# Two norms of a chained FFN and attention block: scaling by the reciprocal root moved from the matmul inputs to the tiles that leave PSUM

## What is computed

```python
h = h + merged @ w_out
hn = rmsnorm(h, norm_ffn_g)
u = causal_dwconv(hn @ w_up, ffn_conv_w, ffn_conv_b)      # 3 taps along time
gate, val = jnp.split(u, 2, axis=-1)
h = h + (jax.nn.silu(gate) * val) @ w_down
x = rmsnorm(h, norm_out_g)                                # end of the first block
h = rms_norm(x, l0_pre_norm)                              # second block, GLA
proj = h @ w_in                    # q, k, v, gate, and 16 rank columns
gk = gk_low @ w_gk2 + b_gk; log_a = log_sigmoid(gk) / 16
```

## Time and profile before

| | |
|---|---|
| median of the runs | 2308.6 us |
| profiled execution, span from first to last instruction | 2306.9 us |
| PE matmul busy | 2207.6 us, 96% |
| DVE, ACT, POOL busy | 56%, 53%, 12% |
| mean granted TensorE clock | 0.979 |
| stage w_out and before, to the last matmul | 0 to 707.4 us |
| stage w_up | 717.2 to 1217 us |
| stage w_down | to 1463.0 us |
| rank tile, gates, GLA heads | 1474.9 to 1789.7 us |

### The profile page before, as it was taken

One profiled execution on the slowest core, in us unless ns is written; L12 is line 12 of the kernel. 1 busy time (PEld: TensorE's weight loads), 2 busy tenths in 40 slices (PEclk: granted clock), 3 DMA queues, 4 the chain that ended last, 5 costly groups with the idle time before them and its releaser, 6 DMA issues.

```text
span 2306.9 us, 47015 instructions
## 1 busy us (share of the span) xinstructions
PE 2207.6 (96%) x17592; PEld 2165.1 (94%) x17592; DVE 1288.3 (56%) x1529; ACT 1214.1 (53%) x1666; POOL 287.2 (12%) x349
## 2 busy tenths in 40 slices
PE   6999999999998999999999999799999988999996
PEld 5999999999997999999999999789999978899996
DVE  5555564444446666666665555555555556655534
ACT  5444445544445666666664444555555444555643
POOL 2000000010112000000001000200100113121111
PEclk7999999999998999999999999899999999999998
DMA  3544545445453555555555555344444433444443
GB/s 144 181 166 166 180 166 185 183 177 192 174 186 138 182 182 182 182 182 182 182 182 201 206 212 197 131 158 171 166 172 174 179 130 132 163 161 145 145 173 118
DMA packets 54923, 393.77 MB, mean 171 GB/s; under 512 B 6097, under 2 KB 6225, under 8 KB 7522
## 3 DMA queue, kind: packets, MB, share of 16 engines
q1 hardware_dynamic: 54432, 392.19, 47.3%
q10 hardware_dynamic: 450, 1.02, 0.1%
HBM read 391.09 MB, written 2.10 MB: 170 GB/s over the span
## 4 chain that ended last, share of the span: by engine, by line
PE 75%; issue 16%; POOL 3%; DVE 3%; ACT 2%; DMA 0%; DVEq 0%; POOLq 0%; ACTq 0%
PE acc L536 22%; PE acc L538 22%; PE acc L537 22%; PE tok L573 2%; PE tok L574 2%; PE tok L575 2%; POOL n_lo L1816 1%; POOL sumsq L1805 1%; PE att L591 1%; POOL sumsq_g L1807 1%; DVE rstd L1302 0%; DVE normed L1316 0%; POOL x L1829 0%; POOL probs L1971 0%; ACT n_hi L897 0%
## 5 line engine op out<-in xcount | busy, mean ns | idle before, releaser
L1294 DVE TENSOR_TENSOR w_lo<-raw,w_hi 128x1024 fp32r<-128x1024 f32 x740 | 912.2, 1246 | 764.4 <-ACT w_hi L874 762.5
L536 PE MATMUL acc<-n_hi,w_hi 128*128 128x256 f32 x3488 | 1002.3, 287 | 42.9 <-POOL n_lo L1816 35.5
L537 PE MATMUL acc<-n_lo,w_hi 128*128 128x256 f32 x3488 | 994.7, 285 | 0.0
L538 PE MATMUL acc<-n_hi,w_lo 128*128 128x256 f32 x3488 | 994.7, 285 | 0.0
L874 ACT ACTIVATE w_hi<-raw 128x1024 fp32r<-128x1024 f32 x740 | 771.5, 1054 | 369.3 <-DMA raw<-stream_in 153.9
L536 PEld LDWEIGHTS acc<-n_hi,w_hi 128*128 128x128 f32 x3488 | 677.5, 194 | 48.1 <-issue 39.9
L537 PEld LDWEIGHTS acc<-n_lo,w_hi 128*128 128x128 f32 x3488 | 677.8, 194 | 0.5
L538 PEld LDWEIGHTS acc<-n_hi,w_lo 128*128 128x128 f32 x3488 | 677.4, 194 | 0.0
L536 PE MATMUL acc<-f_hi,w_hi 128*128 128x256 f32 x688 | 193.6, 281 | 0.0
L537 PE MATMUL acc<-f_lo,w_hi 128*128 128x256 f32 x688 | 193.6, 281 | 0.0
L538 PE MATMUL acc<-f_hi,w_lo 128*128 128x256 f32 x688 | 193.6, 281 | 0.0
(11 more groups left out here) (305 smaller groups left out, 3001.6 us busy)
## 6 DMA issues: line engine op xcount, KB each, us to landing
raw<-stream_in SPq DMA_DIRECT2D x370, 1024.0 KB, 4.8
x<-x_in SPq DMA_DIRECT2D x4, 512.0 KB, 7.5
out<-x SPq DMA_DIRECT2D x4, 512.0 KB, 2.6
v_bias<-v_bias_in ACTq DMA_DIRECT2D x1, 512.0 KB, 8.7
par<-params_in ACTq DMA_DIRECT2D x1, 287.0 KB, 5.5
pos_i<-positions_in ACTq DMA_DIRECT2D x1, 128.0 KB, 6.8
gk<-gk_in ACTq DMA_DIRECT2D x1, 68.0 KB
```

The lines of the kernel that those rows point to most:

```text
L536: nc.tensor.matmul(out, w_hi[:, s, wc], hi[:, k, :], start=first, stop=False)
L537: nc.tensor.matmul(out, w_hi[:, s, wc], lo[:, k, :], start=False, stop=False)
L538: return nc.tensor.matmul(out, w_lo[:, s, wc], hi[:, k, :], start=False, stop=last)
L1294: nc.vector.tensor_tensor(w_lo[:, s, :], raw[:, s, :], w_hi[:, s, :].bitcast(fp32), ALU.subtract).then_inc(lo_ready, 1)
```

## The change

For the FFN norm and for `pre0`, the matmuls take x times the norm's weights, and the reciprocal root is multiplied in when an accumulation leaves PSUM.

- As each x tile is added (w_out, w_down), ACT writes `n_hi` = x times gain, DVE `n_lo` by one operation (`unscaled_low`). PE waits for them tile by tile (`unscaled`). `normed` and POOL's part are gone for these two norms.
- PE puts the sums over partitions between the two units of the next accumulation (`between`).
- In w_up DVE makes `f_pre` = accumulation times `rstd`, and ACT makes `f_gate`, `f_val` from `f_pre`; a new semaphore `flin_ready` tells DVE of it.
- In GLA DVE makes `q_sb`, `k_sb`, `o_sg` and `rank_rows` out of PSUM times `rstd`; Silu is taken by ACT afterwards, in place. v has tokens on partitions, so the root is needed as a column, `rcol`: two matmuls of one column each and a copy.
- The first q tile of head 0 comes ahead of the gate logits. Head 0 is written out ahead of the loop over the other three. ACT and DVE take the gates of head 0 first, and those of heads 1 to 3 after one more weight unit.

The diff, cut to the parts that are spoken of:

```diff
+                        if unscaled is not None:
+                            pe.wait_ge(xlo_ready, UNSCALED[unscaled] * KT + 8 * n + c + 1)
...
+                    if n == 0 and between is not None:
+                        between()
...
-            norm_sum("ffn")
+            feature_tile("wup", 0, 0, 1, 0, n_hi, n_lo, unscaled="ffn", between=lambda: norm_sum("ffn"))
+            feature_tile("wup", 0, 2, 0, 0, n_hi, n_lo)
...
+            def scale_column():
+                pe.wait_ge(rstd_ready, NORM["pre0"] + 1)
+                pe.wait_ge(tok_taken, FREE + 2 * count(3, "gla", 0, 0))
                 for t in range(2):
+                    last = nc.tensor.matmul(tok[0][:, t:t + 1], rstd[0:1, t * P:(t + 1) * P], ones[0:1, 0:1],
+                                            start=True, stop=True)
+                last.then_inc(rcol_made, 1)
...
+            def gla(i):
+                first = isinstance(i, int)
                 for n in range(4):
                     feature_tile("gla", i, 2 * n, n % 2, n // 2, n_hi, n_lo)
+                    if first and n == 0:
+                        scale_column()
+                        gate_logits()
+                if first:
+                    pe.wait_ge(rcol_ready, 1)
...
+                            nc.scalar.activation(n_hi[:, 2 * i + m, :], x[:, 2 * i + m, :], ACT.Identity,
+                                                 scale=scale[:, i, m:m + 1]).then_inc(xhi_ready, 1)
+                        for k in split_after(j, (per // 2 - 1, per - 1)):
+                            split(name, i, k)
...
             def up(i):
                 for j in range(4):
+                    if j == 2:
+                        act.wait_ge(ftap_ready, 2 * i + 1)
+                        act.wait_ge(fact_ready, FREE + i)
+                        nc.scalar.activation(f_silu[:, :], f_gate[:, :], ACT.Silu)\
+                            .then_inc(fsilu_ready, 1)
+                    split("wup", i, j)
                     if j in (1, 3):
                         n = j // 2
-                        unit_is_done("wup", i, j)
+                        taken(act, 1 - n, "wup", i, 0)
                         if n == 0:
                             act.wait_ge(fsilu_ready, FREE + i)
                         else:
                             act.wait_ge(fact_ready, FREE + i)
-                        nc.scalar.activation((f_gate, f_val)[n][:, :], acc[1 - n][:, 0:T], ACT.Identity,
+                        nc.scalar.activation((f_gate, f_val)[n][:, :], f_pre[:, n, :], ACT.Identity,
                                              bias=par_ffn[:, i, 4 * n + 3:4 * n + 4],
-                                             scale=par_ffn[:, i, 4 * n + 2:4 * n + 3])
-                        nc.scalar.activation(f_pre[:, n, :], acc[1 - n][:, 0:T], ACT.Copy)\
-                            .then_inc(acc_taken[1 - n], 1)
-                    if j == 2:
-                        act.wait_ge(ftap_ready, 2 * i + 1)
-                        act.wait_ge(fact_ready, FREE + i)
-                        nc.scalar.activation(f_silu[:, :], f_gate[:, :], ACT.Silu)\
-                            .then_inc(fsilu_ready, 1)
-                    split("wup", i, j)
+                                             scale=par_ffn[:, i, 4 * n + 2:4 * n + 3]).then_inc(flin_ready, 1)
...
+            def gate_logs(heads):
+                for hd in heads:
+                    act.wait_ge(gk_ready, hd + 1)
+                    chain.step(nc.scalar.activation(g_log[:, hd, :], att[hd][:, :], ACT.Abs))
+                chain.wait()
+                for hd in heads:
+                    chain.step(nc.scalar.activation(g_log[:, hd, :], g_log[:, hd, :], ACT.Exp, scale=-1.0))
+                chain.wait()
+                for hd in heads:
+                    nc.scalar.activation(g_log[:, hd, :], g_log[:, hd, :], ACT.Ln, bias=1.0)\
+                        .then_inc(glog_ready, 1)
...
+                    split("gla", i, j)
+                    if j in (17, 19, 21, 23):
+                        n = (j - 17) // 2
+                        taken(act, n % 2, "gla", i, 2 + n // 2)
+                        nc.scalar.activation(o_sg[:, n, :], o_sg[:, n, :], ACT.Silu).then_inc(osg_ready, 1)
...
+            def unscaled_low(n, i, m, scale):
+                at = UNSCALED[n] * KT
+                dve.wait_ge(xhi_ready, 2 * i + (at + m + 1))
+                nc.vector.scalar_tensor_tensor(
+                    out=n_lo[:, 2 * i + m, :], in0=x[:, 2 * i + m, :], scalar=scale[:, i, m:m + 1],
+                    in1=n_hi[:, 2 * i + m, :].bitcast(fp32), op0=ALU.mult, op1=ALU.subtract)\
+                    .then_inc(xlo_ready, 1)
...
             def up(i):
                 for j in range(4):
                     if j in (1, 3):
                         n = j // 2
+                        unit_is_done("wup", i, j)
+                        nc.vector.tensor_tensor(f_pre[:, n, :], acc[1 - n][:, 0:T], rstd[:, :], ALU.mult)\
+                            .then_inc(acc_taken[1 - n], 1)
+                    split("wup", i, j)
+                    if j in (1, 3):
                         u = (f_gate, f_val)[n]
-                        taken(dve, 1 - n, "wup", i, 0)
+                        dve.wait_ge(flin_ready, 2 * i + n + 1)
...
+                    if j in (17, 19, 21, 23):
+                        n = (j - 17) // 2
+                        unit_is_done("gla", i, j)
+                        nc.vector.tensor_tensor(o_sg[:, n, :], acc[n % 2][:, 0:T], rstd[:, :], ALU.mult)\
+                            .then_inc(acc_taken[n % 2], 1)
+                        if n == 3:
+                            split("gla", i, j)
...
+                    if first and j == 1:
+                        gate_sums(0)
+                    if first and j == 2:
+                        for hd in range(1, G_HEADS):
+                            gate_sums(hd)
...
-                        taken(dve, 0, "gla", i, 3)
-                        taken(dve, 1, "gla", i, 3)
+                        dve.wait_ge(osg_ready, 4 * i + 4)
```

More of the change, by code:

```diff
@@ L469, in done, with again @@
                 self.i = None
+            def again(self, i):
+                assert self.n - self.start == self.per, (self.n - self.start, self.per)
+                self.n, self.i = self.start, i
             def step(self, ins):
@@ L687, in _ @@
                         last.then_inc(unit_done, 1)
[L691 to L697, removed]
@@ L700, in _, with norm_sums_out @@
-            taken(pe, 1, "rank", None, 0)
-            pe.wait_ge(gk2_loaded, 16)
-            for hd in range(G_HEADS):
-                for t in range(2):
[L704 to L709, removed]
+            def norm_sums_out():
+                pe.wait_ge(sq_added, FREE + KT * (POOLED["out"] + 1))
+                nc.tensor.matmul(att[3][:, 0:T], ones[:, :], sumsq[:, :], start=True, stop=True)
+                nc.tensor.matmul(att[3][:, T:2 * T], ones[:, :], sumsq_g[:, :], start=True, stop=False)
+                nc.tensor.matmul(att[3][:, T:2 * T], eps_tile[:, :], sumsq[:, :], start=False, stop=True)\
+                    .then_inc(stat_ready, 1)
@@ new lines, in gate_logits @@
+            def gate_logits():
+                taken(pe, 1, "rank", None, 0)
+                pe.wait_ge(gk2_loaded, 16)
+                pe.wait_ge(std_ready, NORM["out"] + 1)
+                for hd in range(G_HEADS):
+                    for t in range(2):
+                        c = (2 * hd + t) * P
+                        last = nc.tensor.matmul(att[hd][:, t * T:(t + 1) * T], gk2[:, c:c + P],
+                                                rank_rows[0:G_RANK + 1, :], start=True, stop=True)
+                    last.then_inc(gk_ready, 1)
@@ L1086, in _ @@
-            nc.scalar.activation(rank_rows[0:G_RANK, :], acc[1][0:G_RANK, 0:T], ACT.Copy)\
-                .then_inc(acc_taken[1], 1)
             split("rank", None, 0)
             split("rank", None, 1)
-            for hd in range(G_HEADS):
-                act.wait_ge(gk_ready, hd + 1)
-                chain.step(nc.scalar.activation(g_log[:, hd, :], att[hd][:, :], ACT.Abs))
-            chain.wait()
-            for hd in range(G_HEADS):
-                chain.step(nc.scalar.activation(g_log[:, hd, :], g_log[:, hd, :], ACT.Exp, scale=-1.0))
@@ L1634, in _ @@
                                                 ALU.subtract).then_inc(oglo_ready_dve, 1)
-                    split("gla", i, j)
-                chain.done(G_HEADS)
+                    else:
+                        split("gla", i, j)
+                    if first and j == 3:
+                        dve.wait_ge(std_ready, NORM["out"] + 1)
+                        nc.vector.reciprocal(out_rstd[:, :], std[:, :]).then_inc(rstd_ready, 1)
+            dve.wait_ge(rcol_ready, 1)
+            dve.wait_ge(at_init, 2)
+            chain.loop(0, 7)
+            gla(0)
+            with dve.Fori(1, G_HEADS) as i:
+                chain.again(i)
+                gla(i)
```

(2 more changed lines are left out.)

146 lines of the change are left out of this document (73 added, 73 removed).

## The result

The changed kernel takes 2257.5 us (median of 4, 2254.5 to 2259.7) against 2308.6 (median of 4, 2306.6 to 2310.6): ratio 0.978, 95% interval 0.976 to 0.979. 2280 was forecast, with 2273 to 2293 as range. The gain is 51 us, not 28.6. Its profiled execution took 2256.7 and has a span of 2255.0.

A forecast was written before the change was run, and what follows sets the result against it. PE, busy 96% of the span, bounds the kernel, so only its waits can be gained: -15.0 (FFN norm) - 18.2 (pre-norm) + 3 (FFN loop) + 1.6 (last head) = -28.6, from 2308.6 to 2280, range 2273 to 2293.

The forecast's parts named there:

- PE's own pace is the yardstick: FFN tiles before the change: 11.51 us each, 23.02 for a loop pass of two, 5.76 for one accumulation of 48 matmuls.
- w_out and w_down: ... covered: In w_out and w_down, one more n_hi (0.45) and n_lo (0.42) per tile fit in the time available, at no cost.
- The FFN norm: Between w_out and w_up: PE goes on without the gap, first accumulation readable at 714.0 against 729.0, gain 15.0.
- The ring: FFN loop: a ring of waits through ACT and DVE takes 23.28 a pass against PE's 23.02; cost 3, bounds 0 to 18.
- the lead: At w_up's start the engines are 3.2 us ahead of PE's need, which the longer loop passes eat first.
- heavy-ring rival: FFN loop: the ring of waits costs 13 instead of 3, giving 2290; chance 0.15.
- The second norm: Pre-norm of the attention after w_down: head 0's fourth tile done at 1503.5 against 1521.7, gain 18.2.
- The chain: Gates of head 0: logits at 1478.0, ACT's work to 1489.7, DVE's to 1495.4, q_sb frees the bank at 1497.0.
- PE's wait for q_sb: Head 0, between third and fourth tile: one new wait of PE on DVE, 3 to 5.6 us.
- The end of the last head: Before the output projection: scaling (0.35) and a low half (1.13) come ahead of o_norm on DVE; cost 1.6, between 0.4 and 3.
- the fall of the clock: At the last head's end, a lower PE clock was counted only in the cost's upper end of 3.
- The last rival: ACT's table loads hold it 2.66 us instead of 1.28, in the FFN loop and the gates' chain: 2314; chance 0.03.

The follow-up runs named there:

- e2: The changed kernel with rcol put at the far end of SBUF, so every other tile keeps its address from before the change: 2282.4 us, ratio 0.989.
- e1: The kernel before with only the tiles behind the fixed ones moved 64 bytes further on in SBUF, without the changed computation: 2286.2 us, ratio 0.990.
- e9: The kernel before with only the FFN norm's part of the change, all tiles at the old addresses: 2295.8 us, ratio 0.9954.
- e7: The changed kernel with w_up's Silu behind the third high half and every PE input at distance 192 modulo 256 from the weights: 2228.6 us, ratio 0.966.
- e13: Inputs at 192 and late Silu on the changed kernel, plus an unread 16-column matmul behind the sum over partitions between w_up's first two units: 2226.7 us.
- e8: The kernel before with every PE input at distance 192 modulo 256 from the weights, nothing of the changed computation: 2235.3 us, ratio 0.972.
- e6: The changed kernel with every PE input at distance 192 modulo 256 from the weights, Silu not moved: 2239.3 us, ratio 0.970.

## Why the prediction was wrong

**The step that failed** is "PE's own pace is the yardstick": the pace of before was taken as given for every stage, and "w_out and w_down: ... covered" stands in the sum with 0. What that term says of the work is right: with n_hi and n_lo added and the old addresses, e2's w_out and w_down take 91.01 and 244.81 us from first to last matmul, the same as before. But the pace moved by 4.5% where an input lies in the region (a part of the merge, w_out, w_down, the first output projection) and by 0.8% in the last projection, for a reason that had nothing to do with the change's idea. e1 gives its size, 22.9 us of 51. The forecast's bounds held only waits and the clock, and a changed address moves neither.

**The FFN norm**, 15.0: measured 14.96 in the trace, and in e9, with the ring, 10.6 in time. w_up starts without a wait, as forecast. Only the first reading of an accumulation is later than reckoned, 8.8 behind w_out's last matmul (698.86) and not 6.7, since 1/root is there at 705.91 only and a low half stands between it and f_pre on DVE; the bank was not wanted before 710.9, so it cost nothing:

```profile
704.16 1.75 DVE L1332 RECIPROCAL rstd<-std 128x256 f32<-128x256 f32 x1 [0.38 <-ACT std L935]
706.53 1.22 DVE L1324 TENSOR_TENSOR w_lo<-raw,w_hi 128x1024 fp32r<-128x1024 f32 x1 [0.62 <-ACT w_hi L919]
707.68 0.42 DVE L1549 TENSOR_TENSOR f_pre<-acc,rstd 128x256 f32<-128x256 f32 x1
```

**The ring**, 3: measured 4.2. A pass was to take 23.28 and takes 23.37, from the first of these rows to the second:

```profile
1082.31 0.38 PE L552 MATMUL acc<-n_hi,w_hi 128*128 128x256 f32 x1
...
1105.68 0.38 PE L552 MATMUL acc<-n_hi,w_hi 128*128 128x256 f32 x1
```

It cost nothing for the first eight passes, until the lead was gone, as forecast. But no wait of PE on w_lo shows in the list, only starts 0.4 apart, once a pass. The heavy-ring rival falls.

**The second norm**, 18.2: measured 17.3, from w_down's last matmul to that of head 0's fourth tile (58.56 before, 41.26 after). The sums now come at 1436.09 with 0.20 of wait in place of 2.85. The chain was the one forecast, ACT (first lines) and DVE (last two):

```profile
1457.70 1.28 ACT L1139 ACT_TABLE_LOAD   x1
1459.00 1.68 ACT L1139 ACTIVATE g_log<-g_log 128x512 f32<-128x512 f32 x3
```

```profile
1465.21 1.20 DVE L1324 TENSOR_TENSOR w_lo<-raw,w_hi 128x1024 fp32r<-128x1024 f32 x1
1466.33 0.42 DVE L1613 TENSOR_TENSOR q_sb<-acc,rstd 128x256 f32<-128x256 f32 x1
```

PE's wait for q_sb was to be 3 to 5.6 and is 3.2. No wait for gk is left. The logits took 3.69 us in place of 6.30, at a granted clock of 1.00. The 0.9 that is missing is mostly the clock behind the wait for q_sb: it was granted at 0.79 from 1467 to 1475, and the fourth tile took 7.22 us from first to last matmul, where the third took 5.64. That is 1.6 lost, where 0.8 was reckoned.

**The end of the last head**, 1.6 with 3 as its upper end: measured 3.4. DVE's queue behind the last output-gate tile, whose last matmul starts at 1742.12, is the one forecast:

```profile
1742.92 1.22 DVE L1324 TENSOR_TENSOR w_lo<-raw,w_hi 128x1024 fp32r<-128x1024 f32 x1
1744.06 0.42 DVE L1625 TENSOR_TENSOR o_sg<-acc,rstd 128x256 f32<-128x256 f32 x1
1744.39 1.21 DVE L1324 TENSOR_TENSOR w_lo<-raw,w_hi 128x1024 fp32r<-128x1024 f32 x1
1745.53 1.22 DVE L1701 TENSOR_TENSOR o_norm<-o_norm,o_sg 128x1024 f32<-128x1024 f32 x1
```

Before, where that matmul starts at 1789.59:

```profile
1791.48 1.21 DVE L1629 TENSOR_TENSOR o_norm<-o_norm,o_sg 128x1024 f32<-128x1024 f32 x1
```

o_norm comes 3.41 behind the matmul in place of 1.89, and the 1.5 between them are the scaling and the low half. Silu is not what it waits for:

```profile
1743.52 1.28 ACT L1176 ACT_TABLE_LOAD   x1
1744.82 0.42 ACT L1176 ACTIVATE o_sg<-o_sg 128x256 f32<-128x256 f32 x1
```

It ends at 1745.24, before the low half does. PE's wait is 3.14 in place of 1.47, 1.7 longer: 1.5 by this chain and 0.2 because PE comes to it sooner at the quicker pace. The mis-sized part is the fall of the clock, which the forecast had only in its upper end: the granted clock was 0.64 between 1750 and 1754, and 1.00 in the four us behind the wait before; this costs 1.7. It doesn't follow from the wait alone: e7 waits 3.1 there as well and keeps 1.00. Why was not looked for.

**The last rival**, loads that hold ACT for 2.66 us: against it, Ln at 1459.00 starts 0.02 behind the end of its load of 1.28. The Trainium skill, "ScalarE: Activation LUTs", section "What ACT_TABLE_LOAD costs", adds a drain to each load, and no run here shows one. The rival had come to 2314.

e2 is the test of the whole: without the shift 2282.4, against the forecast of 2280. So the forecast holds for the change at the old addresses, with a gain of 26.7 and not 28.6.

## A version that beats both

e7, the changed kernel with late Silu and every input at 192: 2228.6 us, ratio to before 0.966 (0.964 to 0.968), 29 under the changed kernel. e13, the same with the useless small matmul, is level with it (0.965). e8 shows that most of this needs no change of the computation: 2235.3 (interval 0.966 to 0.978). e7 is not at the quick pace throughout: its w_up and w_down went at 0.1178, and at 0.1133 they would be some 28 us shorter, by the estimate above. No edit here brought that about.

## What to carry to other kernels

Before the terms of a change are summed, list the addresses of PE's operands in both programs: a new tile of 8 bytes was worth 22.9 us here, and the change itself 26.7. Test the idea and the layout in two separate runs, one with the shift alone, one with the change alone. And where reordering makes one engine's output wait for another's inside a loop, ask for the whole ring: moving one Silu behind a weight half gave back all that the scaling in PSUM had cost w_up.

## What the runs showed of the hardware

- Matmuls of 128x256 that follow each other without a wait, at full granted clock, start 0.1133 to 0.1200 us apart, by the distance modulo 256 bytes between the SBUF addresses of input and weights (table above). Why the distance matters, no run shows.
- At a distance of 192 there are two paces, 0.1133 and 0.1178, for the same instructions and addresses. A row of matmuls keeps its own, for 85 accumulations of w_up in e8, and can change it at a break, as in e6 and e7.
- The last projection had 0.1178 in the changed kernel and in e1, where the first one, with its input at the same addresses, had 0.1133.
- After a wait of PE for og_lo of 3.1 us the granted clock fell to 0.64 for four us in the changed kernel, at a cost of 1.7 us; in e7, after the same wait, it stayed at 1.00.
